# A rebuilt opening for a two-block layer kernel: first projection tiles interleaved, squares behind casts, rope angles in PSUM, and two tiles moved across the index part

## The chip, the cores and the metric

One NeuronCore of one Trainium2 chip runs the whole program once. The metric is the device time of one execution in microseconds (us), as a median of several runs. A difference of under 0.3% (about 4.2 us here) can't be told from no change.

## The reference

The input is one sequence of 512 tokens of width 1024, in float32. A hybrid layer (sparse top-k attention beside a gated convolution, cross attention, a convolutional feed-forward part) and a second layer (a linear recurrence beside stick-breaking attention, a feed-forward part) follow each other. The change touches only the beginning of the first layer:

```python
def hybrid_layer(x, mem, cos, sin, norm_mix_g, w_in, ...):
    h = rmsnorm(x, norm_mix_g)
    proj = h @ w_in
    q, k, v, qi, ki, wi, glu = jnp.split(proj, cuts, axis=-1)
    q = partial_rope(q.reshape(bsz, seq, A_HEADS, HEAD_DIM), cos, sin)
    k = partial_rope(k[:, :, None, :], cos, sin)[:, :, 0]
    qi = partial_rope(qi.reshape(bsz, seq, IDX_HEADS, IDX_DIM), cos, sin)
    ki = partial_rope(ki[:, :, None, :], cos, sin)[:, :, 0]
    a_out = dsa_attention(q, k, v, qi, ki, wi)
```

`cos` and `sin` are those of `position * frequency`. `dsa_attention` scores each key for each query with `qi`, `ki` and `wi` (the "index"), and keeps the 128 best keys of a row.

## The kernel before

**Products in three passes.** A float32 matrix product is made of three fp32r products. ScalarE rounds a weight chunk to `weights_high` (L700 and L689), GpSimd subtracts that from the raw weights to give `weights_low` (L610), and the operand has the parts `a_high` (ScalarE, L714) and `a_low` (VectorE, L1131). A tile of 128 output columns by 512 tokens takes 8 blocks of the inner dimension times 3 passes, 24 matmuls of 128x512, summed in one of the two halves of the PSUM tensor `acc`. Even chunks use weight slot 0 and `acc` half 0, odd ones slot 1 and half 1. Six more PSUM banks are called `aux0` to `aux5`.

**The projection.** `w_in` gives 16 tiles. Tile 0 holds the index's key and weights (`kiwi`), tiles 1 and 2 the index's queries (`qiT`), tile 3 key and value (`kv`), tiles 4 to 11 the gated convolution's input, tiles 12 to 15 the attention's queries. The projection runs on x times its gain, without the root mean square. That factor comes from the sum of the squares of x: ScalarE squares the 8 blocks (`square_x`, L706), VectorE adds them (`add_x`, L1125), TensorE sums over the features (plan step `sum`, L1853), ScalarE takes the root, VectorE the reciprocal, and TensorE spreads it over the partitions (plan step `spread`, L1745). VectorE multiplies it into the tables `sine` and `cosine`. The tables come from the positions: VectorE multiplies by the frequency and subtracts multiples of 2 pi (L1140 to L1149), ScalarE applies its sine (L781, L782).

**The order of the work.** The Python list `FIRST_PLAN` is written out by hand, and the code of each engine walks the same list and takes its own part of each step. So the list sets the order on TensorE, VectorE, ScalarE and GpSimd alike. `("tile", n, k0, k1)` is tile n from inner block k0 to k1. The steps `key_turn`, `query_turn` and `wi` are TensorE's turned copies, `key` and `query` VectorE's rope, `index` one head's scores of one block of queries, `mem_scale` GpSimd's work on the memory. `BETWEEN[n]` is what stands behind tile n; its steps `best` are VectorE's searches for the 8 largest scores. Tiles 0 and 1 are made together by `first_tiles`, ahead of the list's other steps: TensorE takes all 16 products of high with high, then all of `a_low`, then all of `weights_low`:

```python
for k, s in order:
    t_.matmul(acc[:, s], weights_high[...], a_high[:, k], ...)
for k in range(KB):
    for s in range(2):
        t_.matmul(acc[:, s], weights_high[...], a_low[:, k], ...)
for s in range(2):
    for k in range(KB):
        last = t_.matmul(acc[:, s], weights_low[...], a_high[:, k], ...)
    last.then_inc(chunk_done, 1)
```

When a tile is done, ScalarE copies it out of `acc` and rounds the chunk of two tiles on (`tile_ends`, `high_next`), and GpSimd makes that chunk's low part (`low_after`). Before the opening proper, TensorE runs 12 float32 products of a unit matrix (L1756), and GpSimd writes the constants. SyncE issues the loads of the weights (L531, L534, L529), of the 8 blocks of x (L535) and of the memory; ScalarE issues those of the parameters and of the positions, which are broadcast to all 128 partitions (L683).

## Time and profile before

| what | value |
|---|---|
| median of 3 runs | 1393.65 us (1391.83 to 1396.83) |
| the profiled execution: its own time | 1390.86 us |
| the profiled execution: span of its instructions | 1388.7 us |
| TensorE busy, share of the span | 96% |
| VectorE, ScalarE, GpSimd busy | 57%, 39%, 44% |
| mean granted TensorE clock | 0.99 |

The profiled execution lies 2.79 us under the median, and its own time 2.16 us over its span. Times within the program count from the start of the span.

### The profile page before, as it was taken

How to read it: one execution, taken by the hardware profiler on the slowest of the kernel's cores; microseconds unless marked ns; L12 is line 12 of the kernel's file. 1: busy time of each engine (PE TensorE's matmuls, PEld its weight loads, DVE VectorE, ACT ScalarE, POOL GpSimd, SP SyncE). 2: the span in 40 equal slices, each digit the busy share in tenths (PEclk: the TensorE clock that was granted, in tenths of full speed). 3: DMA queues.
4: the chain of work that ended last, by engine and by line, in shares of the span. 5: the costliest groups of instructions: out<-in, count | busy, mean ns of one | idle time of the engine just before them, and what ended most of it. 6: DMA issues, size and time to landing. Idle time of an engine off the chain costs nothing.

```text
span 1388.7 us, 18012 instructions
## 1 busy us (share of the span) xinstructions
PE 1337.5 (96%) x6189; PEld 1083.1 (78%) x6189; DVE 786.7 (57%) x1100; ACT 543.4 (39%) x855; POOL 611.7 (44%) x299
## 2 busy tenths in 40 slices
PE   7998989999999999999999998899999999999997
PEld 5787867787678888888888777677778888888887
DVE  6697897643456777777534588666453333332231
ACT  5454676543243322322223353444442322323322
POOL 4587974432244444444434533122344444444341
PEclk9999999999999999999999999899999999999999
DMA  6122321221122323223332222111122323223322
GB/s 224 46 91 90 114 70 47 76 92 61 46 76 92 105 91 98 98 91 108 104 104 79 89 78 74 46 47 46 61 91 93 104 91 101 95 96 106 103 84 82
DMA packets 31875, 121.19 MB, mean 87 GB/s; under 512 B 3536, under 2 KB 3664, under 8 KB 31568
## 3 DMA queue, kind: packets, MB, share of 16 engines
q1 hardware_dynamic: 31392, 119.55, 25.9%
q10 hardware_dynamic: 432, 0.96, 0.3%
q8 instruction: 32, 0.52, 0.2%
q14 instruction: 19, 0.16, 0.0%
HBM read 118.40 MB, written 2.10 MB: 87 GB/s over the span
## 4 chain that ended last, share of the span: by engine, by line
PE 73%; issue 13%; POOL 5%; DVE 5%; ACT 3%; DMA 1%; POOLq 0%; SPq 0%; ACTq 0%; DVEq 0%
PE acc L1701 60%; POOL weights_low L610 4%; PE acc L1838 3%; PE aux L2090 1%; PE acc L2186 1%; POOL conv L659 1%; PE aux L2070 1%; PE acc L1810 1%; DVE aux L1206 1%; PE aux L1924 1%; ACT weights_high L689 1%; DVE left L1551 1%; PE aux L2080 1%; DVE a_low L1367 1%; DMA weights_raw<-w 1%
## 5 line engine op out<-in xcount | busy, mean ns | idle before, releaser
L610 POOL TENSOR_TENSOR weights_low<-weights_raw,weights_high 128x1024 fp32r<-128x1024 f32 (+1 forms) x204 | 526.1, 2579 | 743.7 <-ACT weights_high L689 741.3
L689 ACT CAST weights_high<-weights_raw 128x1024 fp32r<-128x1024 f32 (+1 forms) x202 | 222.0, 1099 | 507.2 <-PE acc L1701 480.1
L1701 PE MATMUL acc<-a_high,weights_high 128*128 128x512 f32 x976 | 389.8, 399 | 4.5 <-POOL weights_low L610 3.1
L1701 PE MATMUL acc<-a_high,weights_low 128*128 128x512 f32 x976 | 381.1, 390 | 0.0
L1701 PE MATMUL acc<-a_low,weights_high 128*128 128x512 f32 x976 | 380.6, 390 | 0.0
L1701 PEld LDWEIGHTS acc<-a_high,weights_high 128*128 128x128 f32 x976 | 183.7, 188 | 47.0 <-issue 6.4
L1701 PEld LDWEIGHTS acc<-a_low,weights_high 128*128 128x128 f32 x976 | 183.8, 188 | 39.6 <-issue 2.6
L1701 PEld LDWEIGHTS acc<-a_high,weights_low 128*128 128x128 f32 x976 | 183.6, 188 | 38.5
L1179 DVE TENSOR_TENSOR residual<-acc,residual 128x512 f32<-128x512 f32 (+1 forms) x63 | 43.3, 687 | 172.0 <-PE acc L1701 129.8
L1701 PE MATMUL acc<-h_high,weights_high 128*128 128x512 f32 x330 | 129.0, 391 | 0.0
L1701 PE MATMUL acc<-h_high,weights_low 128*128 128x512 f32 x330 | 128.5, 389 | 0.0
L1701 PE MATMUL acc<-h_low,weights_high 128*128 128x512 f32 x330 | 128.5, 389 | 0.0
L1449 DVE TENSOR_TENSOR h_low<-work,h_high 128x512 f32 x44 | 88.9, 2021 | 39.5 <-ACT h_high L930 39.5
L1443 DVE TENSOR_TENSOR work<-acc,row_factor 128x512 f32<-128x512 f32 x44 | 30.4, 691 | 105.4 <-PE acc L1701 105.4
L1701 PEld LDWEIGHTS acc<-h_high,weights_low 128*128 128x128 f32 x330 | 62.0, 188 | 12.9
L1701 PEld LDWEIGHTS acc<-h_high,weights_high 128*128 128x128 f32 x330 | 62.0, 188 | 12.7
L1701 PEld LDWEIGHTS acc<-h_low,weights_high 128*128 128x128 f32 x330 | 62.0, 188 | 12.6
L927 ACT ACTIVATE work<-work 128x512 f32<-128x512 f32 x44 | 27.7, 630 | 96.7 <-DVE work L1440 93.6
L1363 DVE TENSOR_TENSOR square_sum<-square_sum,square 128x512 f32<-128x512 f32 x19 | 50.8, 2676 | 19.4 <-ACT square L1076 9.1
L1206 DVE SCALAR_TENSOR_TENSOR aux<-glu,par,aux 128x512 f32<-128x512 f32 x78 | 58.8, 753 | 1.7
L1438 DVE SCALAR_TENSOR_TENSOR work<-gated,par,work 128x512 f32<-128x512 f32 x22 | 55.4, 2520 | 3.4 <-DVE work L1436 3.4
L659 POOL TENSOR_TENSOR conv<-conv,product 128x512 f32<-128x512 f32 x38 | 49.4, 1299 | 10.4 <-ACT product L763 9.0
(378 smaller groups left out, 1933.2 us busy)
## 6 DMA issues: line engine op xcount, KB each, us to landing
weights_raw<-w SPq DMA_DIRECT2D x172, 512.0 KB, 3.3
weights_raw<-w SPq DMA_DIRECT2D x32, 704.0 KB, 4.1
residual<-xT SPq DMA_DIRECT2D x8, 256.0 KB, 7.6
out<-y_tok SPq DMA_DIRECT2D x4, 512.0 KB, 3.1
mem_raw<-memT SPq DMA_DIRECT2D x1, 1024.0 KB, 5.4
mem_tok<-mem SPq DMA_DIRECT2D x1, 1024.0 KB, 7.4
lru_weights<-blockdiag ACTq DMA_DIRECT2D x1, 512.0 KB, 3.4
sine<-positions ACTq DMA_DIRECT2D x1, 256.0 KB, 7.0
```

Source lines behind the costliest of these rows:

```text
L610: g.tensor_tensor(weights_low[:, s, 0:cols], weights_raw[:, s, 0:cols], weights_high[:, s, 0:cols].bitcast(F32), ALU.subtract).then_inc(we ...
L659: g.tensor_tensor(conv[:, b], conv[:, b], product[:, j % 2], ALU.add).then_inc(last_conv_steps, 1)
L689: a.copy(weights_high[:, s, 0:cols], weights_raw[:, s, 0:cols]).then_inc(weight_high, 1)
L927: a.activation(work[:, 0], work[:, 0], ACT.Silu).then_inc(silu_ready, 1)
L1179: v.tensor_tensor(residual[:, bass.ds(n, 1)].rearrange("p a n -> p (a n)"), acc[:, s], residual[:, bass.ds(n, 1)].rearrange("p a n -> p (a ...
L1206: ins = v.scalar_tensor_tensor(dst, src, weight, sofar, ALU.mult, ALU.add)
L1363: v.tensor_tensor(total_ if to is None else to, total_, squares, ALU.add).then_inc(summed, 1)
L1438: own.then(v.scalar_tensor_tensor(work[:, 0], gated[:, 1:1 + T], dcol("fconv_w", c + 1), work[:, 0], ALU.mult, ALU.add))
L1443: v.tensor_tensor(work[:, 1], acc[:, 1], row_factor[:], ALU.mult).then_inc(tile_out[1], 1)
L1449: v.tensor_tensor(at(dst_low, i), work[:, 1], at(dst_high, i).bitcast(F32), ALU.subtract).then_inc(operand_low, 1)
L1701: last = t_.matmul(acc[:, bank, 0:cols], w[:, s, wide], x_[:, k0 + k, 0:cols], start=start and k == opens and n == 0, stop=stop and k == c ...
L1838: last = t_.matmul(acc[:, t], w[:, q % 2, wide], x_[:, block0 + k], start=k == 0 and n == 0, stop=k == 3 and n == 2)
```

## The change

The change has these parts, all in the first 70 us of the program.

1. `first_tiles` is written in another order: tile 0 gets its low weight products and its `a_low` products between the high ones of both tiles, and ends after 32 matmuls; tile 1's 16 remaining products follow. ScalarE rounds the next chunk as soon as tile 0 is done, before it copies the tile out.
2. On ScalarE most squares of x stand behind the casts of x. They go to eight buffers (a PSUM bank and parts of tiles that are not in use yet), so no square waits for a buffer. VectorE makes all 8 `a_low` first, and adds the squares between the steps of the angles, in the PSUM bank `aux5`.
3. The angles live in the PSUM bank `aux4` (`angle`) until they are reduced. ScalarE applies the sine ahead of the plan's steps, with the sine's table loaded at the very start in place of the root's; the root's is loaded after it.
4. The positions are loaded by SyncE after x, no longer by ScalarE ahead of most of x.
5. In the plan, tiles 2 and 3 stand ahead of the turned keys and queries (tile 3 with gaps of 2, 3 and 3 blocks for `sum` and `spread`), tile 4 stands whole ahead of the index, and tile 5 is cut in four among the index's steps, where tile 4 was. `spread` scales the tables straight from PSUM, and ScalarE makes the copy of `cosine` in `aux4`.

```diff
-        FIRST_PLAN = [("tile", 0, 0, KB), ("tile", 1, 0, KB), ("tile", 2, 0, 4), ("sum",), ("key_turn", 0),
-                      ("spread",), ("wi",), ("query_turn", 0), ("key", 0), ("query", 0), ("tile", 2, 4, KB),
-                      ("mem_scale", 0, 4), ("tile", 3, 0, 4), ("query_turn", 1), ("query", 1),
-                      ("tile", 3, 4, KB), ("mem_scale", 4, 8)]
+        FIRST_PLAN = [("tile", 0, 0, KB), ("tile", 1, 0, KB), ("tile", 2, 0, KB), ("tile", 3, 0, 2), ("sum",),
+                      ("tile", 3, 2, 5), ("spread",), ("key_turn", 0), ("query_turn", 0), ("tile", 3, 5, KB),
+                      ("wi",), ("query_turn", 1), ("mem_scale", 0, 4), ("key", 0), ("query", 0), ("query", 1),
+                      ("tile", 4, 0, KB), ("mem_scale", 4, 8)]
         for n in range(len(INDEX)):
-            FIRST_PLAN += [("index", n)] + ([("tile", 4, 2 * (n // 3), 2 * (n // 3) + 2)] if n % 3 == 2 else [])
+            FIRST_PLAN += [("index", n)] + ([("tile", 5, 2 * (n // 3), 2 * (n // 3) + 2)] if n % 3 == 2 else [])
...
+            sp.dma_start(sine[:].bitcast(I32), positions.partition_broadcast(P)).then_inc(positions_in, 16)
...
-            act.dma_start(sine[:].bitcast(I32), positions.partition_broadcast(P)).then_inc(positions_in, 16)
...
-                if k >= 2:
-                    square_x(k - 2)
-            for k in range(KB - 2, KB):
+                if k in (4, 6):
+                    square_x(k // 2 - 2)
+            for k in range(2, 5):
                 square_x(k)
+            tile_done(0, 0)
+            high_next(0, 0)
+            a.copy(kiwi[:], acc[:, 0]).then_inc(tile_out[0], 1)
+            square_x(5)
+            tile_done(0, 1)
+            high_next(0, 1)
+            a.copy(qiT[:, 0], acc[:, 1]).then_inc(tile_out[1], 1)
+            square_x(6)
+            square_x(7)
+            act.wait_ge(angle_ready, 2)
+            own.step(a.activation(sine[:], sine[:], ACT.Sin))
+            a.activation(cosine[:], cosine[:], ACT.Sin, bias=half_pi, scale=-1.0).then_inc(tables_ready, 1)
+            own.step(a.activation(tok_root[:, 5:6], eps, ACT.Sqrt))
...
-                if k >= 3:
-                    add_x(k - 2)
-            add_x(KB - 2)
-            add_x(KB - 1)
-
             dve.wait_ge(positions_in, 16)
             own.then(v.tensor_copy(cosine[:], sine[:].bitcast(I32)))
-            own.then(v.tensor_scalar(sine[:], cosine[:], col("freq"), None, ALU.mult))
-            own.then(v.tensor_scalar(cosine[:], sine[:], float(1 / (2 * np.pi)), ROUND, ALU.mult, ALU.add))
+            own.then(v.tensor_scalar(angle, cosine[:], col("freq"), None, ALU.mult))
+            add_x(1)
+            own.then(v.tensor_scalar(cosine[:], angle, float(1 / (2 * np.pi)), ROUND, ALU.mult, ALU.add))
             own.then(v.tensor_scalar(cosine[:], cosine[:], -ROUND, None, ALU.add))
-            for piece in TWO_PI:
-                own.then(v.scalar_tensor_tensor(sine[:], cosine[:], -piece, sine[:], ALU.mult, ALU.add))
-            v.tensor_scalar(sine[:], sine[:], 3.1415925, -3.1415925, ALU.min, ALU.max
-                            ).then_inc(angle_ready, 1)
+            add_x(2)
+            for n, piece in enumerate(TWO_PI):
+                own.then(v.scalar_tensor_tensor(angle, cosine[:], -piece, angle, ALU.mult, ALU.add))
+                if n < 2:
+                    add_x(3 + n)
+            v.tensor_scalar(sine[:], angle, 3.1415925, -3.1415925, ALU.min, ALU.max).then_inc(angle_ready, 1)
...
+                part(0, 0, 0)
+                part(0, 1, 0)
+                part(0, 0, 2)
+                part(0, 1, 2)
+                part(1, 0, 0)
+                part(1, 1, 0)
+                for k in range(2, KB):
+                    part(0, k, 0)
+                    part(1, k, 0)
+                    part(0, k, 2)
+                    part(0, k - 2, 1)
+                part(0, KB - 2, 1)
+                part(0, KB - 1, 1).then_inc(chunk_done, 1)
                 for k in range(KB):
+                    part(1, k, 1)
+                for k in range(KB):
+                    last = part(1, k, 2)
+                last.then_inc(chunk_done, 1)
```

Here `part(s, k, which)` is one matmul of tile s and block k: 0 is high with high, 1 is the high weights with `a_low`, 2 the low weights with `a_high`.

**TensorE, the first two tiles.** Before, behind the 12 products of the unit matrix:

```order
L1765 MATMUL acc<-a_high,weights_high 128x512 [waits operand_high,weight_high] x15
L1770 MATMUL acc<-a_low,weights_high 128x512 [waits operand_low]
...
L1775 MATMUL acc<-a_high,weights_low 128x512 [waits weight_low]
L1775 MATMUL acc<-a_high,weights_low 128x512 x7
L1701 MATMUL acc<-a_high,weights_high 128x512 [waits weight_low,tile_out0]
```

and with the change, where the rows left out repeat the four before them for the blocks 4 to 7:

```order
L1787 MATMUL acc<-a_high,weights_high 128x512 [waits operand_high,weight_high]
L1787 MATMUL acc<-a_high,weights_low 128x512 [waits operand_high,weight_low] x2
L1787 MATMUL acc<-a_high,weights_high 128x512 [waits operand_high,weight_high] x4
L1787 MATMUL acc<-a_high,weights_low 128x512 [waits operand_high,weight_low]
L1787 MATMUL acc<-a_low,weights_high 128x512 [waits operand_low,weight_high]
...
L1787 MATMUL acc<-a_low,weights_high 128x512 [waits operand_low,weight_high] x11
L1787 MATMUL acc<-a_high,weights_low 128x512 [waits operand_high,weight_low] x8
L1719 MATMUL acc<-a_high,weights_high 128x512 [waits weight_low,tile_out0]
```

The third matmul now needs the first chunk's low part, and the tenth needs the first `a_low`; before, the first 16 needed neither.

**VectorE, from the last `a_low` to the tables** (`sine` arrives with the positions, `gate`, `score` and `product` hold squares of x). Before:

```order
L1125 TENSOR_TENSOR square_sum<-square_sum,gate 128x512 [waits x_summed,x_squared] x3
L1140 CAST cosine<-sine 128x512 [waits positions_in]
L1141 TENSOR_SCALAR sine<-cosine,par 128x512 [waits dve_steps]
L1142 TENSOR_SCALAR cosine<-sine 128x512 [waits dve_steps]
L1143 TENSOR_SCALAR cosine<-cosine 128x512 [waits dve_steps]
L1145 SCALAR_TENSOR_TENSOR sine<-cosine,sine 128x512 [waits dve_steps] x3
L1146 TENSOR_SCALAR sine<-sine 128x512 [waits dve_steps]
L1149 SCALAR_TENSOR_TENSOR cosine<-sine 128x512 [waits angle_ready]
```

and with the change:

```order
L1151 TENSOR_SCALAR aux<-cosine,par 128x512 [waits dve_steps]
L1139 TENSOR_TENSOR aux<-aux,gate 128x512 [waits x_squared,dve_steps]
L1153 TENSOR_SCALAR cosine<-aux 128x512
L1154 TENSOR_SCALAR cosine<-cosine 128x512 [waits dve_steps]
...
L1157 SCALAR_TENSOR_TENSOR aux<-cosine,aux 128x512
L1160 TENSOR_SCALAR sine<-aux 128x512 [waits dve_steps]
L1162 SCALAR_TENSOR_TENSOR cosine<-sine 128x512 [waits angle_ready]
L1139 TENSOR_TENSOR aux<-aux,score 128x512 [waits x_summed,x_squared] x2
L1139 TENSOR_TENSOR square_sum<-aux,product 128x512 [waits x_summed,x_squared]
```

The sum of squares now ends behind the angles, not ahead of them, and most steps have one operand in PSUM.

**TensorE, around the factor.** Before, in one run without a tile's matmul between them:

```order
L1853 MATMUL aux<-ones,square_sum 128x1 [waits x_summed]
L1853 MATMUL aux<-ones,square_sum 128x1 x3
L1864 MATMUL aux<-kiwi,twice 128x512 [waits tile_out0]
L1865 MATMUL aux<-kiwi,rotate_twice 128x512
L1745 MATMUL aux<-ident,small 128x128 [waits x_factor]
L1745 MATMUL aux<-ident,small 128x128 x3
L1787 MATMUL aux<-ident,kiwi 128x128 [waits row_ready]
L1787 MATMUL aux<-ident,kiwi 128x128 x3
L1872 MATMUL aux<-qiT,rotate 128x512 [waits tile_out1]
```

and with the change, where each row left out is a tile's matmul or a repeat of the row above:

```order
L1884 MATMUL aux<-ones,square_sum 128x1 [waits x_summed]
...
L1763 MATMUL aux<-ident,small 128x128 [waits x_factor]
...
L1895 MATMUL aux<-kiwi,twice 128x512 [waits tile_out0]
L1896 MATMUL aux<-kiwi,rotate_twice 128x512
L1903 MATMUL aux<-qiT,rotate 128x512 [waits tile_out1]
...
L1818 MATMUL aux<-ident,kiwi 128x128 [waits row_ready]
```

Nine matmuls of tile 3 now stand between the sum and the spread, and nine more between the turned query and `wi`; before, only the turned key stood behind the sum, and nothing between the spread and `wi`.

## Rows read from the trace of the kernel before

**Rows 1.** The page's shares by engine, and its chain that ended last.

```profile
PE 1337.5 (96%) x6189; PEld 1083.1 (78%) x6189; DVE 786.7 (57%) x1100; ACT 543.4 (39%) x855; POOL 611.7 (44%) x299
...
PE 73%; issue 13%; POOL 5%; DVE 5%; ACT 3%; DMA 1%; POOLq 0%; SPq 0%; ACTq 0%; DVEq 0%
```

**Rows 2.** Timeline of TensorE, its idle times: start, us, work [idle before <-releaser].

```profile
7.92 0.47 PE L1765 MATMUL acc<-a_high,weights_high 128*128 128x512 f32 x1 [0.90 <-ACT a_high L714]
9.91 0.47 PE L1765 MATMUL acc<-a_high,weights_high 128*128 128x512 f32 x1 [1.52 <-ACT a_high L714]
11.39 7.08 PE L1765 MATMUL acc<-a_high,weights_high 128*128 128x512 f32 x14 [1.00 <-ACT weights_high L700]
28.57 0.47 PE L1701 MATMUL acc<-a_high,weights_high 128*128 128x512 f32 x1 [2.85 <-POOL weights_low L610]
35.61 0.66 PE L1787 MATMUL aux<-ident,kiwi 128*128 128x128 f32 x4 [0.78 <-DVE row_factor L1216]
```

**Rows 3.** The chain that ended last, in order of time: start, us, what.

```profile
37.13 5.48 PE acc L1701 x24
...
58.12 6.82 PE acc L1701 x30
...
67.44 10.92 PE acc L1701 x48
```

**Rows 4.** Stretches: busy (instructions) of PE, PEld, DVE, ACT, POOL; granted clock, DMA share, GB/s.

```profile
4.50:7.00 2.50, 2.50 (x12) 2.22 (x11) 0.00 (x0) 1.04 (x1) 1.70 (x7) 1.00 0.93 158
7.00:10.46 3.46, 0.96 (x3) 0.37 (x2) 2.39 (x2) 1.61 (x3) 2.18 (x1) 1.00 1.01 377
10.46:17.28 6.82, 5.89 (x12) 3.13 (x12) 5.38 (x7) 6.82 (x12) 2.37 (x1) 0.50 0.96 360
25.70:28.60 2.90, 0.05 (x2) 0.06 (x1) 2.87 (x2) 1.53 (x2) 2.90 (x2) 1.00 0.00 0
```

**Rows 5.** Timeline of ScalarE.

```profile
11.24 0.72 ACT L714 ACTIVATE a_high<-residual,par 128x512 fp32r<-128x512 f32 x1
11.87 0.61 ACT L706 ACTIVATE gate<-residual 128x512 f32<-128x512 f32 x1
24.43 1.05 ACT L689 CAST weights_high<-weights_raw 128x1024 fp32r<-128x1024 f32 x1
32.66 1.28 ACT L781 ACT_TABLE_LOAD   x1
```

**Rows 6.** Timeline of GpSimd.

```profile
6.84 2.35 POOL L610 TENSOR_TENSOR weights_low<-weights_raw,weights_high 128x1024 fp32r<-128x1024 f32 x1
11.41 2.37 POOL L610 TENSOR_TENSOR weights_low<-weights_raw,weights_high 128x1024 fp32r<-128x1024 f32 x1 [2.23 <-ACT weights_high L700]
25.55 5.40 POOL L610 TENSOR_TENSOR weights_low<-weights_raw,weights_high 128x1024 fp32r<-128x1024 f32 x2 [11.77 <-ACT weights_high L689]
```

**Rows 7.** Groups of VectorE up to 60 us, by form: busy, mean ns | idle before.

```profile
L1131 DVE SCALAR_TENSOR_TENSOR a_low<-residual,par,a_high 128x512 fp32r<-128x512 f32 x8 | 8.5, 1068 | 6.8 <-ACT a_high L714 6.6
L1149 DVE SCALAR_TENSOR_TENSOR cosine<-sine 128x512 f32<-128x512 f32 x1 | 2.8, 2764 | 0.0
L1146 DVE TENSOR_SCALAR sine<-sine 128x512 f32<-128x512 f32 x1 | 2.5, 2450 | 0.0
L1248 DVE TENSOR_SCALAR score<-aux,wi 128x512 f32<-128x512 f32 x1 | 0.8, 752 | 0.3 <-ACT aux L799 0.3
L1143 DVE TENSOR_SCALAR cosine<-cosine 128x512 f32<-128x512 f32 x1 | 0.4, 428 | 0.0
```

**Rows 8.** Timeline of VectorE: an `a_low`, and its idle times behind the index.

```profile
12.06 2.94 DVE L1131 SCALAR_TENSOR_TENSOR a_low<-residual,par,a_high 128x512 fp32r<-128x512 f32 x2 [1.44 <-ACT a_high L714]
...
59.59 0.70 DVE L1256 TENSOR_TENSOR score<-score,causal 128x128 f32<-128x128 f32 x3
...
66.89 0.70 DVE L1169 TENSOR_TENSOR aux<-aux,sine 128x512 f32<-128x512 f32 x1 [3.64 <-PE aux L1865]
...
109.65 0.70 DVE L1160 TENSOR_TENSOR aux<-aux,sine 128x512 f32<-128x512 f32 x1 [4.91 <-PE aux L1872]
115.99 0.70 DVE L1160 TENSOR_TENSOR aux<-aux,sine 128x512 f32<-128x512 f32 x1 [1.24 <-PE aux L1872]
```

More of the change, by code:

```diff
@@ L767, in _ @@
                 j = n[0] if n else 0
-                if what == "tile" and n[2] == KB:
+                if what == "tile" and n[2] == KB and j >= 2:
                     tile_ends(j)
@@ L779, in _ @@
                 elif what == "spread":
[L780 to L783 removed]
+                    act.wait_ge(table_scaled, 1)
+                    a.copy(aux[4][:], cosine[:]).then_inc(table_copied, 1)
                 elif what == "mem_high":
```

63 lines of the change are left out of this document (31 added, 32 removed).

## The prediction

> **What bounds the kernel now.** I read the page's shares first: TensorE is busy for 96% of the span and holds 73% of the chain that ended last [rows 1]. So time is won only where TensorE idles or runs slowly. Its timeline has five idle times before 60 us: 0.90, 1.52, 1.00, 2.85 and 0.78 us, 7.05 in all [rows 2]. The table of stretches adds what idleness doesn't show. From 10.46 to 17.28 us the granted clock is 0.50, that is 1.2 GHz in place of 2.4, behind a stretch (7.00 to 10.46) in which TensorE was busy for 0.96 of 3.46 us [rows 4]. At full clock a 128x512 matmul costs 5.48 / 24 = 0.228 us [rows 3]. Tiles 0 and 1 are 48 matmuls, 10.9 us of work, and they last from 7.92 to 28.57 - 2.85 = 25.72 [rows 2], 17.8 us. From 28.57 to 67.44, where tile 6 starts [rows 3], TensorE idles for 0.78 us only [rows 2], so that stretch holds 38.1 us of work. The change must therefore be read from two numbers: when tile 2 starts (28.57) and when tile 6 starts (67.44). Both plans have done the same work by tile 6; behind it they are identical.
>
> **Tile 0's start.** ScalarE rounds a weight chunk in 1.05 us, a block of x in 0.72, with the next instruction 0.63 behind its start, and a square takes 0.61 more [rows 5]; without squares between, 6 blocks need 3.8 us and x keeps ahead of TensorE. Before, x came late: from 4.50 to 7.00 the DMA engines were 93% busy but moved 158 GB/s, against 377 right after [rows 4], while the broadcast of the positions was in flight. Moving it behind x lets the first two blocks and the second chunk land earlier, I estimate by 1 to 2.5 us. The first matmul then goes when the warm-up products end, 7.02 (7.92 - 0.90) [rows 2]: 0.9 us earlier. The third matmul needs the first low weights, ready at 9.19 [rows 6]; it goes at 9.33, since I allow 0.14 us for the hand-over. GpSimd's second subtraction follows at once, 0.5 us late because of the `a_low` that waits, and ends at about 12.05 (before: 11.41 + 2.37 = 13.78 [rows 6]).
>
> **The wait on `a_low`.** The eight `a_low` take 1068 ns on average [rows 7], because some met GpSimd's subtraction: the one at 12.06 and its follower last 2.94 us and end at 15.00 [rows 8], only 1.22 past GpSimd's end at 13.78 [rows 6]. So the first waits out the subtraction and runs its last 0.55 us behind it, and a free one adds about 0.66. The same shows at the angles: 2450 and 2764 ns beside the two subtractions from 25.55 [rows 6, 7], where a step of the first kind takes 428 ns alone [rows 7]. By that rule the first `a_low` is ready at 9.73, the second at 12.6, the others every 0.66 us to 16.6. The Trainium skill (SBUF - State Buffer, section Who interferes with whom) calls this an exclusive lock on a shared port pair; the trace agrees, by the 2450 ns above.
>
> In the new order the high products and the low weights run from 9.33 at 0.228 us each, the fourteenth matmul waits for the second `a_low` until 12.75 (0.9 us lost), and tile 0 ends with the last `a_low` at 17.1. Tile 1's 16 remaining matmuls end at 20.7, against 25.72: **5.0 us earlier**. If the second chunk lands no earlier than before, this end moves by 0.9 us.
>
> **Tile 2's start.** Before, it waited 2.85 us for its low weights [rows 2]: copy out, cast, subtraction all behind tile 0's late end. Now tile 0 ends 16 matmuls (3.6 us) before tile 1: cast 17.2 to 18.25, subtraction 2.4 us to 20.75, start at 20.9. That is **7.7 us earlier** than 28.57; 0.2 of the 2.85 us is left.
>
> **The sum of squares.** The price of this is a later sum. VectorE's chain behind the last `a_low`: 0.45 for the cast (428 ns for its neighbour of that form [rows 7], and the hand-over), then at 0.75 us the steps with a PSUM operand, the nearest row being a `TENSOR_SCALAR` from PSUM with 752 ns [rows 7]; the step that stays in SBUF (`cosine<-cosine`) meets the subtraction of 18.35 to 20.75 and ends at 21.0; then 8 instructions of 0.72 give the angles at 26.75, and three additions that wait for each other, 0.79 with the hand-over, the sum at 29.1. TensorE wants it after 30 matmuls of tiles 2 and 3, at 20.9 + 6.8 = 27.7. That is a new wait of **1.4 us**. Bounds: 0 if the SBUF step slips in ahead of the subtraction (chain 1.9 us shorter), and 3.5 if another instruction is held for 2 us. I take 1.4. The VectorE steps themselves hide beside TensorE. Here a page speaks against the change: the Trainium skill (VectorE: DVE Perf Modes, section Why PSUM operands drop a tier) says a PSUM operand forbids the doubled float32 rate. The trace agrees (752 against 428 ns); it costs three angle steps about 0.3 us each, which the chain above has, by the rows.
>
> **The factor and the turned tiles.** The wait of 0.78 us for `row_factor` [rows 2] goes: nine matmuls of tile 3 (2.0 us) cover root and reciprocal, and nine more (2.0 us) with turned key and query (2.8 us) cover the scaling, 2.1 us. ScalarE's table load of 1.28 us [rows 5] stands ahead of tile 2's copy instead; the cast for tile 4 then ends near 31, its low weights near 33.5, and tile 4 starts at about 38, so 4.5 us of cover are left. Behind the index, the turned key of `kv` needs all index scores, with only 6 matmuls between: VectorE finished them 1.47 us behind TensorE (59.59 against 58.12) [rows 3, 8], the six take 1.37: 0.1 us lost.
>
> **The sum.** Tile 6 starts at 20.9 + 38.1 + 1.4 + 0.1 = 60.5, against 67.44: **6.9 us gained**.
>
> **Does it reach the end?** VectorE's searches now begin behind tile 5, not before most of it. Before, they began at 59.59, 7.85 us ahead of tile 6, and VectorE then idled 3.64 us for the turned key [rows 8]. Now TensorE has 1.37 us of tile 5, 0.1 of waiting and the turned key and values (67.44 - 64.94 = 2.5 [rows 3]) behind the last score, and VectorE begins 1.47 us behind that score, so 2.5 us ahead of tile 6: 5.35 us later against TensorE. The 3.64 absorb most, and it is 1.7 us late at the key. It idles for another 4.91 and 1.24 us before turned queries [rows 8], so 4.4 us stay free, and the gain passes on. Everything behind waits on events, not on fixed times.
>
> Against the profiled execution: 1390.86 - 6.9 = 1384.0. The median stands 2.79 above that execution, so 1393.65 - 6.9 = 1386.8. New runs may fall a little towards the first count, so I give **1386.6**.
>
> **Rivals.**
>
> *The clock falls in the new opening* (0.15). For it: TensorE still idles from 7.75 to 9.33 and at 11.8. Against it: it is busy for 1.6 us of that stretch, not 0.96. If the half clock lasts 6.82 us again [rows 4], 15 matmuls run in it at 0.456 us and tile 0's other 10 behind it, so tile 0 ends at 19.6 and tile 2 starts at 23.4. The wait for the sum vanishes, and tile 6 starts at 61.6: 5.8 us gained, 1387.8. The Trainium skill (TensorE: Matmul & The Clock Gate, section What's actually happening) has the low clock as the default that activity releases; the 0.50 behind the idle stretch agrees.
>
> *The gain is mostly lost on VectorE* (0.16, within 0.3%). If two more instructions of the chain meet a subtraction (2 us each), the sum costs 4 us more; or if the searches run 4 us longer than the free 4.4. Then 3 us are left, 1390.7. For it: six subtractions lie in this stretch. Against it: only two instructions left have two SBUF operands or the fast form.
>
> *The order does nothing, TensorE waits elsewhere* (0.04). Casts would stay late as x lands: gain 1 us, 1392.6. The idle 2.85 us speaks against it.
>
> *Slower: ScalarE stands at the angles* (0.03). ScalarE's queue now waits for the angles ahead of tile 2's copy and tile 4's cast. Cover is 4.5 us, so it decides once the angles come later than 31.2; each us beyond is a us on TensorE. To be slower by 0.3% they must come at 26.75 + 4.5 + 6.9 + 4.2 = 42.4 or later: 1397.9. VectorE would have to be held through six subtractions.
>
> **Numbers.** The forecast has 0.62, with its own range 1384 to 1389. Low end: the sum's wait gone, 1.4 more, and a median 2 us under that of the three runs shown: 1382.5. High end: the second rival, 1390.8. Faster is under 1389.5, with 0.62 + 0.15 and a little less for the scatter of the medians: 0.76. Within 0.3%: 0.21. Slower: 0.03.
>
> **What would show it.** In the profile after: first matmul at about 7.0; a wait on `a_low` near 12; tile 2 at 20.9 with under 0.5 us of wait on `weights_low`; a wait of 0 to 3.5 us at the sum; none at `row_factor`; tile 6 at 60.5; VectorE's idle time before the turned query 2 shrunk from 4.91 to about 3.2. The forecast is wrong if tile 6 starts early but the turned queries find VectorE busy, or if the granted clock is 0.50 in other places behind.

## The result, and the profile after

| | before | after |
|---|---|---|
| median | 1393.65 us (7 runs, 1391.27 to 1396.83) | **1383.96 us** (7 runs, 1381.46 to 1386.88) |
| ratio | | 0.9926, 95% interval 0.9912 to 0.9939 |
| the profiled execution: own time, span | 1390.86, 1388.7 us | 1384.94, 1382.8 us |
| tile 2 starts | 28.57 us | 21.83 us |
| tile 6 starts | 67.44 us | 60.01 us |

The change takes 9.7 us off the median, the two profiled executions are only 5.92 us apart, and tile 6 starts 7.43 us earlier. These three numbers must fit together, and below they do.

The timeline of TensorE in the changed kernel, its idle times in the opening and what follows them (start, us, work, idle time before and its releaser), to be laid beside [rows 2]:

```profile
6.81 0.47 PE L1787 MATMUL acc<-a_high,weights_high 128*128 128x512 f32 x1 [0.39 <-POOL ident L611]
7.72 0.47 PE L1787 MATMUL acc<-a_high,weights_high 128*128 128x512 f32 x1 [0.43 <-ACT a_high L718]
9.26 1.22 PE L1787 MATMUL acc<-a_high,weights_low 128*128 128x512 f32 x2 [1.08 <-POOL weights_low L617]
...
17.04 2.66 PE L1787 MATMUL acc<-a_low,weights_high 128*128 128x512 f32 x11
19.53 1.98 PE L1787 MATMUL acc<-a_high,weights_low 128*128 128x512 f32 x8
21.83 0.47 PE L1719 MATMUL acc<-a_high,weights_high 128*128 128x512 f32 x1 [0.33 <-POOL weights_low L617]
...
28.72 0.95 PE L1884 MATMUL aux<-ones,square_sum 128*128 128x1 f32 x8
```

The wait of 2.85 us ahead of tile 2 has shrunk to 0.33, and nothing is idle at the sum of squares (28.72) or at the factor. The stretches show the granted clock (busy and instructions of PE, PEld, DVE, ACT, POOL; granted clock; DMA share; GB/s), beside [rows 4]:

```profile
4.50:7.00 2.50, 2.11 (x13) 1.92 (x12) 0.19 (x1) 1.86 (x3) 1.70 (x7) 1.00 0.97 313
7.00:9.06 2.06, 0.75 (x2) 0.19 (x1) 2.06 (x1) 1.51 (x2) 2.06 (x1) 1.00 1.03 383
9.06:12.47 3.41, 3.21 (x8) 2.55 (x9) 3.41 (x3) 3.41 (x7) 2.89 (x2) 0.50 1.06 410
...
21.83:60.01 38.18, 38.08 (x153) 26.96 (x154) 25.25 (x48) 18.30 (x34) 18.19 (x13) 1.00 0.21 70
```

While x lands, the DMA engines now move 313 GB/s, not 158 at nearly the same busy share (97% and 93%). The clock is still 0.50 for a while (1.2 GHz), for 3.41 us in place of 6.83. From tile 2 to tile 6 TensorE idles for 0.10 of 38.18 us.

The gain is not the same all along the program. Steps of both kernels, laid side by side, are 7.35 us apart at 102 us of the changed kernel, 7.60 at 773, 6.41 at 778, 8.34 at 983 and 5.88 at 990. Where it drops, the clock has fallen in the changed kernel alone. The stretch behind 983 us in the kernel before, in the changed kernel, and in `x_squares_between` (below):

```profile
991.61 0.50 PE L1838 MATMUL acc<-y_high,weights_high 128*128 128x512 f32 x1 [2.87 <-DVE residual L1179]
990.20:997.03 6.83, 5.27 (x22) 4.00 (x23) 2.47 (x4) 1.13 (x3) 2.39 (x1) 1.00 0.22 77
```

```profile
983.27 0.79 PE L1869 MATMUL acc<-y_high,weights_high 128*128 128x512 f32 x1 [2.87 <-DVE residual L1195]
981.86:988.69 6.83, 5.42 (x13) 4.27 (x14) 1.77 (x3) 0.98 (x2) 2.36 (x1) 0.50 0.24 77
```

```profile
982.28 0.51 PE L1866 MATMUL acc<-y_high,weights_high 128*128 128x512 f32 x1 [2.87 <-DVE residual L1192]
978.00:987.00 9.00, 5.82 (x24) 4.35 (x24) 4.79 (x9) 2.44 (x4) 2.39 (x1) 1.00 0.16 54
```

The wait is 2.87 us in all three, and the clock is 0.50 in one of them only. That costs 2.5 us there (8.34 less 5.88), and 3.41 us at 0.50 from 773.65 cost 1.2. Between them 1.9 us come back, most of it around 877 us, where the kernel before is at 0.50 for 10.24 us and the changed kernel for 3.41 (and for 3.41 more at 859). So 7.43 us at tile 6 become 5.92 at the end of this pair.

### The profile page after: what moved, and what is told of

Its sections match the earlier page's. It is cut to its first block, busy times and chain, and to the rows that moved or that the text cites. A ratio compares the mean times of both kernels' runs of the same rounds, so it can differ in the third digit from the quotient of the medians.

```text
span 1382.8 us, 18050 instructions
## 1 busy us (share of the span) xinstructions
PE 1337.6 (97%) x6189; PEld 1085.0 (78%) x6189; DVE 784.6 (57%) x1099; ACT 542.9 (39%) x856; POOL 611.1 (44%) x299
## 4 chain that ended last, share of the span: by engine, by line
PE 74%; issue 13%; POOL 5%; DVE 4%; ACT 3%; POOLq 0%; ACTq 0%; DVEq 0%
PE acc L1719 61%; POOL weights_low L617 4%; PE acc L1869 3%; PE aux L2121 1%; PE acc L2217 1%; PE aux L2101 1%; POOL conv L666 1%; PE acc L1841 1%; DVE aux L1222 1%; PE aux L1955 1%; ACT weights_high L695 1%; PE acc L1787 1%; DVE a_low L1385 1%; PE aux L1936 1%; PE aux L2111 1%
## 5 line engine op out<-in xcount | busy, mean ns | idle before, releaser
L1719 PEld LDWEIGHTS acc<-h_low,weights_high 128*128 128x128 f32 x330 | 62.0, 188 | 12.7
L1719 PEld LDWEIGHTS acc<-h_high,weights_high 128*128 128x128 f32 x330 | 62.0, 188 | 12.6
```

Source lines behind the costliest of these rows:

```text
L1719: last = t_.matmul(acc[:, bank, 0:cols], w[:, s, wide], x_[:, k0 + k, 0:cols], start=start and k == opens and n == 0, stop=stop and k == c ...
```

## The experiments

One table holds what all fourteen profiled executions say at the two places that the prediction named. "Clock" is the mean granted clock of the stretch; "wait at the sum" is TensorE's idle time before `ones,square_sum`.

| kernel | tile 2 starts | clock from 6 us to there | wait at the sum | tile 2 to tile 6 | clock in it | tile 6 starts |
|---|---|---|---|---|---|---|
| before | 28.57 | 0.85 | 0 | 38.87 | 1.00 | 67.44 |
| x_before_again | 28.66 | 0.85 | 0 | 40.45 | 0.96 | 69.11 |
| after | 21.83 | 0.89 | 0 | 38.18 | 1.00 | 60.01 |
| x_after_again | 22.11 | 0.89 | 0 | 38.21 | 1.00 | 60.32 |
| x_positions_early | 24.22 | 0.81 | 0 | 38.20 | 1.00 | 62.42 |
| x_tiles_in_passes | 24.47 | 0.91 | 0 | 39.83 | 0.96 | 64.30 |
| x_plan_before | 20.95 | 1.00 | 4.87 | 50.03 | 0.86 | 70.98 |
| x_plan_before_filled | 21.07 | 1.00 | 0.39 | 49.06 | 0.90 | 70.13 |
| x_only_plan | 28.63 | 0.85 | 0 | 39.84 | 0.96 | 68.47 |
| x_angles_sbuf | 21.33 | 1.00 | 1.51 | 41.59 | 0.96 | 62.92 |
| x_squares_between | 21.23 | 1.00 | 0.76 | 39.24 | 1.00 | 60.47 |
| x_hold_clock | 20.95 | 1.00 | 0.75 | 39.25 | 1.00 | 60.20 |
| x_consts_later | 20.52 | 1.00 | 0.86 | 39.33 | 1.00 | 59.85 |
| x_both | 20.44 | 1.00 | 0.85 | 39.32 | 1.00 | 59.76 |

### x_plan_before: the new opening, the old plan

```diff
-        FIRST_PLAN = [..., ("tile", 2, 0, KB), ("tile", 3, 0, 2), ("sum",), ("tile", 3, 2, 5), ("spread",), ...
+        FIRST_PLAN = [..., ("tile", 2, 0, 4), ("sum",), ("key_turn", 0), ("spread",), ("wi",), ...
```

> The changed kernel with the plan of before (half of tile 2, then the sum of squares, then the turned key at once; tile 4 cut up in the index). My theory: the opening gives tile 2's start at 21.83 as in the changed kernel, but the sum of squares is wanted after 12 matmuls, at 24.6, while VectorE has it only at 27.9 (the changed kernel's time): TensorE waits about 3.3 us there, and the 0.78 us wait for row_factor of the kernel before returns. So at the place where tile 6's first matmul starts the plan is worth about 4 us of the 7.4 gained: tile 6 at 63.5 to 64.5. Rival: the plan only moves work about, the sum comes in time or the wait is made good within the index, which was held by VectorE's scores; tile 6 at 60.0 to 60.8.

Measured: median 1394.28 us (10 runs), ratio to the kernel before 1.0011 (0.9996 to 1.0027). **The whole gain is gone**, though tile 2 starts at 20.95, earlier than in the changed kernel. My theory had the direction, but put at 4 us what is 10.97 (tile 6 at 70.98, not 64); the rival (60.0 to 60.8) falls. The timeline of TensorE in this run:

```profile
28.79 1.87 PE L1883 MATMUL aux<-ones,square_sum 128*128 128x1 f32 x8 [4.87 <-DVE square_sum L1138]
...
37.38 1.11 PE L1817 MATMUL aux<-ident,kiwi 128*128 128x128 f32 x4 [1.98 <-DVE row_factor L1234]
```

and two of its stretches:

```profile
23.90:28.80 4.90, 0.03 (x2) 0.01 (x1) 4.62 (x9) 2.22 (x3) 0.56 (x1) 0.86 0.32 112
28.80:41.20 12.40, 10.42 (x25) 6.22 (x26) 4.55 (x11) 1.36 (x4) 0.00 (x0) 0.50 0.00 0
```

The new opening moves TensorE 7.6 us forward (20.95 against 28.57), and VectorE's sum of squares 6.5 us back. It ended at 22.26 us in the kernel before, as this row of VectorE's timeline there says, and ends at 28.7 here:

```profile
19.98 2.28 DVE L1125 TENSOR_TENSOR square_sum<-square_sum,gate 128x512 f32<-128x512 f32 x3
```

So the old plan stands 4.87 us at the sum, and 1.98 at the factor. What I had not priced is the second of the stretches: the clock is 0.50 for 12.4 us, in which TensorE is busy for 10.42. At full clock that work would be about half as long, so I estimate 5.2 us lost. 4.87 + 1.98 + 5.2 = 12.05, against the measured excess over the changed kernel's stretch, 50.03 - 38.18 = 11.85. Nothing is left over for where tiles 4 and 5 stand, which no run changes alone.

### x_only_plan: the old opening, the new plan

```diff
-        FIRST_PLAN = [..., ("tile", 2, 0, 4), ("sum",), ("key_turn", 0), ("spread",), ("wi",), ...
+        FIRST_PLAN = [..., ("tile", 2, 0, KB), ("tile", 3, 0, 2), ("sum",), ("tile", 3, 2, 5), ("spread",), ...
```

> The kernel before with only the new plan (sum of squares behind two matmul groups of tile 3, factor and turned tiles later, tile 5 cut up in the index, tile 5's rest ahead of the turned key). The opening is that of before, so tile 2 starts at 28.6. My theory: the plan alone takes away the 0.78 us wait for row_factor and the few tenths in the index, and nothing else, since with the old opening the sum of squares was ready in time: tile 6 starts 0.8 to 1.2 us earlier than 67.44, at 66.2 to 66.7. Together with the run that has the new opening and the old plan this shows whether the parts add: my theory says they do not (the plan is worth about 4 us behind the new opening, about 1 us behind the old one). Rival: the parts add, so the plan is worth the same here as there.

Measured: median 1391.62 us (10 runs) against 1393.82, ratio 0.9983 (0.9970 to 0.9996). Tile 6 starts at 68.47, not 66.2 to 66.7, because behind the wait of 2.85 us the clock was 0.50 for 3.41 us (clock 0.96 in the table). The second run of the kernel before had the same behind its 2.81 us and shows 69.11; against that one the plan is worth 0.64 us, and its stretch is 40.45 - 39.84 = 0.61 us shorter, near the 0.78 of the factor's wait. **The parts don't add**: the plan alone gives 2.2 us at the median, less than the 4.2 us that can be told apart, the opening alone nothing, both together 9.7.

### x_plan_before_filled: how much of it is the clock

```diff
                 elif what == "sum":
+                    for _ in range(20):
+                        t_.matmul(aux[0][:, 0:P], ident[:], ident[:], start=True, stop=True)
                     pe.wait_ge(x_summed, KB - 1)
```

> The new opening with the plan of before, and with 20 float32 products of the identity with itself on TensorE ahead of the sum of squares (they compute nothing that is used, about 0.22 us each, 4.4 us of the 4.87 us that TensorE waited there in the run without them). It tells apart the two halves of that run's loss. In that run TensorE reached tile 6 at 70.98, 50.0 us behind tile 2's start (20.95); the changed kernel needs 38.2 us (60.01 - 21.83). The 11.9 us between are 4.87 + 1.98 us of waits and, I hold, 5.0 us for the granted clock of 0.50 from 27.48 to 41.13. Theory: with TensorE kept busy the clock stays at 1.00 there, the waits stay, and tile 6 starts 45 to 46 us behind tile 2, that is 5 us earlier, near 66.0; the median is 4 to 5 us under 1394.28. Rival one: the clock falls all the same, as the first and the second wait still leave gaps; tile 6 near 71. Rival two: the second wait, for row_factor, is what counts: it grows by what the clock gives back (to 3 to 4 us), and tile 6 starts at 68 to 69.

Measured: median 1391.95 us (12 runs), 2.3 us under the run without fillers, where I expected 4 to 5; ratio to before 0.9992 (0.9980 to 1.0003). The stretches:

```profile
23.90:28.80 4.90, 4.62 (x41) 4.43 (x39) 4.62 (x8) 2.10 (x3) 0.64 (x1) 1.00 0.34 112
28.80:35.00 6.20, 4.59 (x16) 2.35 (x16) 1.84 (x7) 1.03 (x4) 0.00 (x0) 0.69 0.00 0
35.00:41.20 6.20, 5.71 (x14) 4.01 (x15) 4.50 (x9) 0.45 (x1) 0.00 (x0) 0.50 0.00 1
```

The fillers hold the clock at 1.00 as long as they run. Then it falls all the same, at 31.15 (before: 27.48), around the second wait, which is 1.98 us again. So rival one is nearest: tile 6 at 70.13, 0.85 us won. The 2.3 us between the medians are more than that, but under what can be told apart. The 5 us of low clock are seen in the trace; this run didn't give them back, so what they would be worth alone stays open.

### x_tiles_in_passes: the old order of the first 48 products

```diff
-                part(0, 0, 0)
...
-                for k in range(KB):
-                    last = part(1, k, 2)
+                for k, s in [(0, 0), (1, 0), (0, 1), (1, 1)] + [(k, s) for k in range(2, KB) for s in range(2)]:
+                    part(s, k, 0)
+                for k in range(KB):
+                    for s in range(2):
+                        part(s, k, 1)
+                for s in range(2):
+                    for k in range(KB):
+                        last = part(s, k, 2)
```

> The changed kernel, with the first two tiles' 48 products in the old order: all high products of both, then all with a_low, then all with the low weights. My theory says that the interleaving buys tile 0's early end and so the early low weights of tile 2: here tile 0 ends eight matmuls (1.8 us) before tile 1, not 16, and tile 1's end stays bound by the eight a_low (last ready at 16.5) plus the matmuls behind them: tile 0 ends at about 19 to 20, tile 1 at about 21 to 22, tile 2's low weights need 4.0 to 4.4 us behind tile 0's end (copy and cast 1.5, subtraction 2.5), so tile 2 starts at 23.0 to 24.5 with 1.5 to 2.9 us of wait on weights_low. Tile 6 then starts 1.2 to 2.7 us later than 60.0. Rival: what counts is that ScalarE casts before it squares and that the broadcast is out of the way; then the order of the products changes nothing and tile 2 starts at 21.8 to 22.2.

Measured: 1386.13 us (4 runs), ratio to before 0.9946 (0.9930 to 0.9963). Its timeline of TensorE:

```profile
18.74 3.79 PE L1787 MATMUL acc<-a_high,weights_low 128*128 128x512 f32 x16
24.47 0.47 PE L1719 MATMUL acc<-a_high,weights_high 128*128 128x512 f32 x1 [1.94 <-POOL weights_low L617]
```

Tile 2 at 24.47 with 1.94 us on `weights_low`, inside both expectations: the interleaving is worth 2.6 us there. All 16 products with low weights stand at the end, so tile 0 is done only 8 matmuls before tile 1. Tile 6 starts 4.3 us later than in the changed kernel, not 1.2 to 2.7: behind the 1.94 us the clock was 0.50 for 3.41 us, which cost 39.83 - 38.18 = 1.65 more.

### x_positions_early: the broadcast ahead of x again

```diff
-            sp.dma_start(sine[:].bitcast(I32), positions.partition_broadcast(P)).then_inc(positions_in, 16)
...
+            act.dma_start(sine[:].bitcast(I32), positions.partition_broadcast(P)).then_inc(positions_in, 16)
```

> The changed kernel, with the positions' broadcast back on ScalarE's queue ahead of x. My theory: the broadcast takes the DMA engines while x loads, so the first weight chunk and the first block of x are in place about as before (first matmul at 7.0 to 7.9 us) but the later blocks come 1 to 2 us later; in the new order that is late only where a cast of x is awaited, so tile 0 ends 0.5 to 1.5 us later than the 17.9 us of the changed kernel, and tile 2 starts at 22.4 to 23.3 instead of 21.83. Rival: the DMA engines deliver x in the same time whatever else is in flight; then ScalarE's casts start where they do in the changed kernel and tile 2 starts at 21.8. A third possibility is that only VectorE gains, as the positions come earlier: its angles would then be ready before 25.7, which nothing waits for. Whole time: at most 1.5 us above the changed kernel.

Measured: 1385.16 us (1 run), tile 2 at 24.22, 2.4 us later, more than the 0.5 to 1.5 expected. The stretches of this run:

```profile
4.50:7.00 2.50, 2.17 (x12) 1.97 (x11) 0.00 (x0) 1.05 (x2) 1.70 (x7) 1.00 0.99 175
7.00:9.56 2.56, 0.47 (x1) 0.19 (x1) 1.70 (x1) 1.13 (x2) 2.19 (x1) 1.00 0.97 370
9.56:16.39 6.83, 6.37 (x15) 4.64 (x16) 5.17 (x7) 6.33 (x11) 2.38 (x1) 0.50 0.93 349
```

The DMA engines are 99% busy and move 175 GB/s while the broadcast is among their packets, 313 without it. The second block of x is rounded at 9.15 us instead of 6.85, TensorE is busy for 0.47 of 2.56 us, and then the clock is 0.50 for 6.83 us, as long as in the kernel before. The rival (no effect) falls, and so does the third possibility: the angles are ready at 28.3 us, not before 25.7. In the whole time nothing can be seen of the 2.4 us (1385.16 beside 1384.94 for the profiled execution of the changed kernel): both have places at 0.50 further back, and not the same ones.

### x_angles_sbuf: the angle in SBUF again

```diff
-        angle = aux[4][:]
+        angle = sine[:]
```

> The changed kernel with the angle in the SBUF tile sine, as before. Its steps with two SBUF operands, or in the doubled rate, are then held by GpSimd's subtractions (18.35 to 25.15). My theory: one to three steps wait 2 to 2.5 us each, the steps not held run 0.3 us shorter each, so the angles are ready 0 to 4 us later than 25.7, and the sum of squares between 27.9 and 31.5; TensorE wants the sum at 28.7, so a wait of 0 to 2.8 us shows there, tile 6 starts as much later than 60.0. Rival: the shorter steps win: angles ready at 24 to 25.5, no wait at the sum, tile 6 at 60.0 and no difference in the whole time.

Measured: 1387.73 us (1 run). VectorE's timeline has the cause:

```profile
19.58 2.16 DVE L1157 SCALAR_TENSOR_TENSOR sine<-cosine,sine 128x512 f32<-128x512 f32 x1
...
22.38 2.75 DVE L1157 SCALAR_TENSOR_TENSOR sine<-cosine,sine 128x512 f32<-128x512 f32 x1
```

A subtraction by GpSimd runs from 18.53 to 21.18 us and the next one from 22.18. The same step from PSUM takes 0.69 us beside them. The sum comes at 29.9 and TensorE waits 1.51 us for it. From tile 2 to tile 6 it takes 3.4 us longer than in the changed kernel: 1.5 for the wait, 1.7 for 3.41 us at clock 0.50 from 32.28. Tile 6 starts at 62.92. My theory's range for the wait (0 to 2.8) holds, the rival falls. The Trainium skill (SBUF — State Buffer, section Who interferes with whom) says that a VectorE instruction with two SBUF inputs contends with a GpSimd instruction that reads SBUF, and one with at most one such input outside the fast modes doesn't; 2.16 and 2.75 us against 0.69 agree.

### x_squares_between: squares between the casts again

```diff
-                if k in (4, 6):
-                    square_x(k // 2 - 2)
-            for k in range(2, 5):
-                square_x(k)
+                if k >= 2:
+                    square_x(k - 2)
+            square_x(6)
+            square_x(7)
```

> The changed kernel with ScalarE's squares again between its casts of x (the buffers stay as changed). Each block then takes ScalarE about 1.25 us instead of 0.63. My theory: in the new opening tile 0's high products are held by the slower casts: block 7 is cast at about 16.0 instead of 12.8, the a_low of it comes 0.66 us behind; the a_low chain ended at 16.5 anyway, so tile 0 ends 0.3 to 1.5 us later than 17.9, tile 2 starts at 22.1 to 23.3 and the angles and the sum of squares are as much later at most. Rival: the a_low chain on VectorE alone sets tile 0's end; then TensorE merely waits elsewhere, tile 2 starts at 21.8, and the casts ahead of the squares are worth nothing.

Measured: 1381.58 us (1 run). Here **my theory falls**. The clock stayed at 1.00 in this opening, so it is to be compared with the three other profiles of which that is true and whose opening is the changed kernel's to the last `a_low` (`x_plan_before`, `x_plan_before_filled`, `x_angles_sbuf`): they start tile 2 at 20.95, 21.07 and 21.33. A block takes ScalarE 1.14 us with its square and the last is rounded at 15.7, but tile 2 starts at 21.23, among them, and tile 6 at 60.47. The `a_low`, 0.66 us apart and the last ready at 16.5 in both kernels, set the end of tile 0. The slack is small: the last `a_low` starts at 15.8. This part of the change is worth nothing that these runs can show.

### x_hold_clock, x_consts_later, x_both: is there more in the opening?

Fillers in TensorE's gaps:

```diff
                 part(0, 0, 0)
+                busy(1)
                 part(0, 1, 0)
+                busy(3)
                 part(0, 0, 2)
```

where `busy(n)` runs n products of the unit matrix into `aux0`.

> The changed kernel plus four float32 products of the identity with itself in the opening's gaps (one between the first two products, three before the first with low weights), which compute nothing that is used. They take TensorE no time that it would not have idled, except the last one's tail (up to 0.2 us). My theory: the granted clock falls to 0.50 between 9.1 and 12.5 us in the changed kernel because TensorE idled for most of 6.8 to 9.3; with the gap filled it stays at 1.00 there, and 9 to 12 us holds up to 7 more matmuls. But tile 0 ends with the last a_low, ready at 16.5, so only 0.3 to 0.9 us of it reach tile 2: start at 20.9 to 21.5. Rival one: the clock stays at 0.50 all the same, tile 2 at 21.8 to 22.0. Rival two: the clock is full but the last a_low sets all, tile 2 at 21.8.

Three constants of GpSimd behind its first two subtractions:

```diff
-            pe.wait_ge(consts_ready, NCONST - 1)
+            pe.wait_ge(consts_ready, NCONST - 3)
...
                 elif what == "sum":
+                    pe.wait_ge(consts_ready, NCONST - 1)
```

> The changed kernel with three of GpSimd's constants (two masks and the narrow identity, 1.2 us of GpSimd) built behind its first two subtractions instead of ahead of them; TensorE waits for all constants only at the sum of squares. My theory: the chain of the opening starts at GpSimd: its first subtraction begins at 6.84 now because of the constants, and would begin at about 6.05 (when the first weight chunk is rounded); the first low weights come at 8.5 instead of 9.26, the first a_low 0.7 us earlier too, so tile 0's end, tile 1's end and tile 2's start are all 0.5 to 0.8 us earlier: tile 2 at 21.0 to 21.3, tile 6 at 59.2 to 59.5. Rival: the warm-up products and x's arrival hold the opening (x's first blocks land at about 6.3), and nothing moves by more than 0.2 us.

Both edits together:

> The changed kernel with both additions: filler products in the opening's gaps and three constants behind the first two subtractions. Theory: the two add, as one shortens the chain and the other keeps the clock full along it: tile 2 starts at 20.4 to 20.9 against 21.83, tile 6 at 58.7 to 59.2, and the whole time is 0.9 to 1.4 us under the changed kernel, too little to be certain of by timing, so the milestones decide. Rival: the sum of squares, now wanted 1 us earlier, is waited for and takes back what the opening gives; tile 6 at 59.7 to 60.0.

Measured: 1386.73 and 1381.20 us (1 run each), and 1384.02 us for both (6 runs) beside 1384.15 for the changed kernel (6 runs) in the same set. All three have the clock at 1.00 and start tile 2 at 20.95, 20.52 and 20.44 us, 0.9 to 1.4 us earlier than in the changed kernel. That the fillers did this is not shown: the second has none, and the three profiles named above kept the clock at 1.00 without them and start tile 2 at 20.95 to 21.33. Against those the constants give 0.4 to 0.8 us (the expectation for them, 21.0 to 21.3, was short), the fillers at most 0.4. At most 0.25 us of it reaches tile 6 (60.20, 59.85, 59.76 against 60.01): the rival of the third expectation is right, and tile 6 came neither at 59.2 to 59.5 nor at 58.7 to 59.2, as the second and third theory had it. The timelines of TensorE and VectorE in the first of them:

```profile
28.78 1.05 PE L1891 MATMUL aux<-ones,square_sum 128*128 128x1 f32 x8 [0.75 <-DVE square_sum L1139]
```

```profile
18.31 0.68 DVE L1153 TENSOR_SCALAR cosine<-aux 128x512 f32<-128x512 f32 x1
...
19.02 2.06 DVE L1154 TENSOR_SCALAR cosine<-cosine 128x512 f32<-128x512 f32 x1
```

and that of VectorE and GpSimd in the changed kernel:

```profile
19.00 0.43 DVE L1154 TENSOR_SCALAR cosine<-cosine 128x512 f32<-128x512 f32 x1
...
24.18 1.52 DVE L1162 SCALAR_TENSOR_TENSOR cosine<-sine 128x512 f32<-128x512 f32 x1
...
27.22 0.69 DVE L1139 TENSOR_TENSOR square_sum<-aux,product 128x512 f32<-128x512 f32 x1
```

```profile
19.12 2.56 POOL L617 TENSOR_TENSOR weights_low<-weights_raw,weights_high 128x1024 fp32r<-128x1024 f32 x1 [7.13 <-ACT weights_high L695]
```

The step `cosine<-cosine` works within SBUF. In the changed kernel the low clock delays tile 0's end, so GpSimd's subtraction begins at 19.12, 0.12 us behind that step, which runs in 0.43 us. With a full clock the subtraction begins at 18.40, and the step is held for 2.06. The sum of squares then ends about 0.8 us later (its last addition starts at 28.04, not 27.22), and TensorE, 0.9 us earlier, waits. So the sum is the next bound here: a faster opening pays only with the sum a few matmuls further back, which was not tried.

### x_before_again, x_after_again: why 9.7 us and not 5.9

> The kernel before against itself. Both theories: ratio 1.000. What it tells is how far equal kernels' medians lie apart (I expect under 1.5 us), as a measure for the gap between the 9.7 us by which the medians differ and the 7.4 to 7.6 us by which the two traces do.

> The changed kernel again. Theory one: the gain of the opening is 7.4 to 7.6 us and the rest of the 9.7 is scatter, from the places where the granted clock is 0.50 in a run; then the ratio is about 0.9946, a gain of 6.5 to 8.5 us. Theory two: behind the opening something more is gained on average, as fewer stretches at 0.50; then the gain is again 9 to 10.5 us, and the records of this run show fewer microseconds at 0.50 than those of the kernel before.

Measured: the kernel before against itself 1.0002 (0.9992 to 1.0011), medians 1.1 us apart; the changed kernel 0.9939 (0.9925 to 0.9954), 8.4 us. By the size of the gain that is theory one, at its upper end; but both sets together leave 8.4 to 9.7 us where the profiled pair has 5.9 (6.9 in this set, with 8.8 at tile 6). So I sorted the timed runs by their mean granted clock:

| mean granted clock of the run, and their mean time | before (72 runs of four sets) | after (13 runs) |
|---|---|---|
| 0.988 | 1393.12 (24 runs) | 1387.74 (1 run) |
| 0.990 | 1391.31 (15 runs) | 1385.59 (4 runs) |
| median of all | 1393.44 at 0.988 | 1383.97 at 0.992 |

At one clock the kernels are 5.4 to 5.7 us apart, as the profiled pair (both at 0.990) is with 5.92. The rest of the 9.5 us is that the changed kernel usually runs at a higher mean clock; a line through the 72 runs gives 1.1 us for each 0.001. But a part of that clock is the opening's own doing: it has 3.41 us less at 0.50, which is 0.0012 of the mean, by that line 1.4 us. So the opening is worth about 7 us, as the 7.43 at tile 6 say, and some 2.5 us of the 9.5 are a higher clock behind it; that is an estimate. So the core of theory two holds. Its sign in the records, fewer microseconds at 0.50, is missing from the profiled executions: 31.3 and 31.4 us after, 29.0 and 32.4 before. Both profiles of the changed kernel are at 0.990, below its median of 0.992, so they don't show a typical execution. Two places can be named. The first is in the table of the experiments: behind the wait of 2.8 us ahead of tile 2 the clock was 0.50 for 3.41 us in two of three profiles of the old opening, and in neither of the changed kernel, which has no such wait. The stretch of `x_before_again`:

```profile
28.98:32.39 3.41, 3.41 (x10) 2.64 (x9) 2.75 (x3) 0.00 (x0) 2.05 (x1) 0.50 0.53 167
```

That is worth 40.45 - 38.87 = 1.6 us when it happens. The second are the stretches at 773.65 and 981.86 us shown above, 1.2 and 2.5 us. `x_squares_between`, at 0.994, has neither: it starts tile 6 0.46 us later than the changed kernel and is 3.4 us ahead of it at 990 us. `x_only_plan`, with the old opening, has the one at 982 too, so these falls are not peculiar to the change. Whether the change makes them rarer, or only the draw of 13 runs did, stays open.

## Why the prediction was right, and where it was off

The forecast was 1386.6 us, the range 1382.5 to 1390.8; 1383.96 lies in it, nearer the low end. The mechanism up to tile 6 held with errors of 0.5 to 1 us; that the median is met within 2.6 us is partly luck, as the last step shows. By its own steps:

- **Tile 0's start.** First matmul 7.02, measured 6.81; third 9.33, measured 9.26 (7.72 and 9.53 in the second profile); GpSimd's second subtraction ends at 12.05, measured 11.99. Held. The broadcast's price is confirmed by its own run, though not within my 1 to 2.5 us alone: it also lengthens the low clock.
- **The wait on `a_low`.** The rule "first 9.73, second 12.6, then every 0.66" gave the last at 16.6; measured: two of 2.9 us from 6.81, the last ready at 16.5. Held. No idle time showed near 12, since TensorE, at half clock, was itself late there. In five of the profiles at full clock it shows, as 0.2 to 0.7 us before 12.7 to 13.4 us, where 0.9 was forecast.
- **Tile 0's and 1's end.** 17.1 and 20.7 forecast, about 17.9 and 21.5 measured. The step that failed is the clock: I took 1.00 and gave the fall 0.15. It fell, for half the length that this rival had. My ground against it, 1.6 us of work in that stretch, was wrong: TensorE was busy for 0.75 of 2.06 us (7.00 to 9.06). It fell in both profiles of the changed kernel and in none of the three others with this opening; those start tile 2 at 20.95 to 21.33 us, so the step was right but for the clock.
- **Tile 2's start.** 20.9 with 0.2 us of wait forecast, 21.83 with 0.33 measured, 6.74 us gained in place of 7.7.
- **The sum of squares.** Forecast 29.1 and a new wait of 1.4 us; measured about 27.9 and none. Of the terms up to tile 6 this one was mis-sized most. The lower bound came true by the very case it named: the step `cosine<-cosine` slipped in ahead of the subtraction. A later step, `cosine<-sine`, was held for 1.52 us instead. In the four kernels with the new plan, the angle in PSUM and a full clock the step was caught, and a wait of 0.75 to 0.86 us appeared. So the two errors are one: the clock cost 0.5 to 0.9 us at tile 2, and the delay saved a wait of about 0.8. That they cancel is luck, not foresight.
- **The factor and the turned tiles.** The wait of 0.78 us is gone. At the turned key of `kv` 0.1 us was forecast, about 0.26 measured (last matmul at 56.95 plus 0.228, next at 57.44).
- **The sum of the steps.** Tile 6 at 60.5 forecast, 60.01 measured: 7.43 us in place of 6.9.
- **To the end.** VectorE's idle time before turned query 2 shrinks from 4.91 to 4.04 us (3.2 forecast), and that step runs at 102.30 against 109.65, 7.35 us earlier. So far the gain passes on, as the row shows:

```profile
102.30 0.70 DVE L1176 TENSOR_TENSOR aux<-aux,sine 128x512 f32<-128x512 f32 x1 [4.04 <-PE aux L1903]
```

Further back it does not pass on whole. The forecast named as a sign of being wrong that the clock is 0.50 in other places behind, and in both profiles of the changed kernel it is, at 773.65 to 774.03 and at 981.86 to 982.24 us, while both profiles of the kernel before do the same work at 1.00. That sign came true. I had no term for it; in the profiled pair it turns 7.43 us into 5.92. The wait of 2.87 us ahead of the second place is the same in both kernels, and `x_squares_between` and `x_both` have neither fall, so they may be scatter; their cause is not shown.

- **From the sum to the median.** Here the forecast was least founded. I took the median's 2.79 us over the profiled execution as a fixed distance. It goes with the clock: 0.988 at before's median, 0.990 in its profiled execution, 0.992 at the median after. The opening gives about 7 us and a higher clock behind it the rest of the 9.5; I had no term for that.

Of the rivals, "the order does nothing" and "ScalarE stands at the angles" fell: the old order costs 2.6 us at tile 2, and the angles came at 25.7, far from 31.2. "Mostly lost on VectorE" didn't happen: two instructions more would have had to be held, and it was one (`cosine<-sine`, by 0.8 us) in place of `cosine<-cosine`. What takes all of the gain under the old plan is another mechanism, a sum that is wanted too early. Two parts of the change were never tried alone: ScalarE's rounding ahead of its copy, and the sine ahead of the plan.

## What to carry to other kernels

An earlier start pays only as far as the next operand that another engine makes: here a new opening without the new plan was worth nothing and the plan alone 2 us, so test parts of a change together and apart before one is dropped. Price a wait of TensorE at its length plus what the work behind it may lose at half clock (in some executions 1.6 us behind a wait of 2.8, about 5 us around waits of 4.9 and 2.0). Before a difference of some us is put down to a step, compare the runs' mean clocks, and take off what the step itself does to them. A single profile of each kernel doesn't do for a difference of 1 us: the same opening started tile 2 anywhere from 20.95 to 22.11 us. Where two engines contend for SBUF, a step 0.1 us earlier or later can cost 1.6 us, so a chain with such steps should be wanted late.

## What the runs showed that I had not expected

- The clock's fall follows idle time, but not in every execution: behind 2.85 us of idling it stayed at 1.00 in the first profile and was 0.50 for 3.41 us in two others. In the run with fillers (`x_plan_before_filled`) it fell at 31.15, after TensorE had idled for 0.39 us in the 7 us before.
- The broadcast of 256 KB about halves what the DMA engines deliver while it runs: 158 and 175 GB/s at 93% and 99% busy, against 313 at 97%.
- A VectorE step held by GpSimd's subtraction ended 0.3 to 0.6 us behind it (19.02 + 2.06 = 21.08 against 18.40 + 2.40 = 20.80; 22.38 + 2.75 = 25.13 against 22.18 + 2.40 = 24.58). Where VectorE was first, by 0.12 us, its step kept its 0.43 us and the subtraction took 2.56 instead of 2.40.
